# Token columns in tiles of 512, 260 and 260 instead of three of 344, in a two-layer hybrid decoder step

## The reference

```python
def _layer(h, p_l, lst, w, lb, pos, wbuf, prompt):
    u = _rmsnorm(h, w['norm1_g']) @ w['w_in']
    ...
    y_a, h_new, conv_new = _rglru(a_x, a_g, h0, conv0, ...)
    ...
    y_c, s_new = _hgrn2(c_q, c_f, c_i, c_g, lb, s0, w['hgrn_norm_g'])
    y_d, c_new, n_new, m_new = _mlstm(d_q, d_k, d_v, d_o, d_i, d_f, ...)
    h = h + jnp.concatenate([y_a, y_b, y_c, y_d], axis=-1) @ w['w_out']
    f = _rmsnorm(h, w['norm2_g']) @ w['w_up']
    h = h + jnp.square(jax.nn.relu(f)) @ w['w_down']
    h = h + jax.nn.sigmoid(h @ w['w_ple_gate']) * (p_l @ w['w_ple_proj'])
    return h, (h_new, conv_new, k_new, v_new, s_new, c_new, n_new, m_new)
```

## Time and profile before

| | |
|---|---|
| median of 3 runs | 3236.26 us |
| lowest, highest | 3226.01, 3238.97 us |
| span of the profiled execution | 3234.4 us |
| PE busy | 2971.1 us, 92% |
| DVE, ACT, POOL busy | 1149.4, 905.8, 905.2 us |
| chain that ended last | PE 81%, DVE 11%, ACT 3%, no instruction ready (issue) 3% |
| mean granted TensorE clock | 0.935 |

### The profile page before, as it was taken

One profiled execution on the slowest core, in us unless ns is written; L12 is line 12 of the kernel. 1 busy time (PEld: TensorE's weight loads), 2 busy tenths in 40 slices (PEclk: granted clock), 3 DMA queues, 4 the chain that ended last, 5 costly groups with the idle time before them and its releaser, 6 DMA issues.

```text
span 3234.4 us, 43899 instructions
## 1 busy us (share of the span) xinstructions
PE 2971.1 (92%) x18128; PEld 2801.4 (87%) x18128; DVE 1149.4 (36%) x2022; ACT 905.8 (28%) x1377; POOL 905.2 (28%) x591
## 2 busy tenths in 40 slices
PE   5988977889999999999968899778899999999999
PEld 4887865579999999999967788655899999999998
DVE  4643255553222222222355423566422222222223
ACT  4443222233111111113345332223331111111133
POOL 2111244222222332225131112432122223222251
PEclk8999976789999999999979999768899999999999
DMA  4010100021111111112210111000211111111112
GB/s 165 33 48 27 59 20 7 9 88 40 49 50 45 45 45 49 42 46 69 79 59 23 46 41 58 14 1 9 94 44 49 46 45 45 49 48 45 63 52 79
DMA packets 42756, 155.78 MB, mean 48 GB/s; under 512 B 6786, under 2 KB 8066, under 8 KB 41088
## 3 DMA queue, kind: packets, MB, share of 16 engines
q1 hardware_dynamic: 33696, 125.68, 11.3%
q10 hardware_dynamic: 8928, 28.28, 2.3%
HBM read 136.18 MB, written 17.76 MB: 48 GB/s over the span
## 4 chain that ended last, share of the span: by engine, by line
PE 81%; DVE 11%; ACT 3%; issue 3%; POOL 2%; DMA 0%; ACTq 0%; DVEq 0%; SPq 0%; POOLq 0%
PE pj L338 24%; PE pj L339 24%; PE pj L340 24%; DVE small L1648 2%; DVE ext L1334 2%; DVE ext L1843 1%; PE pm L351 1%; DVE small L1334 1%; PE pj L579 1%; DVE vt L1334 1%; PE pm L545 1%; PE pm L430 1%; POOL w_lo L1190 1%; PE pm L549 1%; PE pm L531 1%
## 5 line engine op out<-in xcount | busy, mean ns | idle before, releaser
L338 PE MATMUL pj<-m_hi,w_hi 128*128 128x344 f32 x1920 | 614.4, 320 | 0.0
L340 PE MATMUL pj<-m_hi,w_lo 128*128 128x344 f32 x1920 | 613.2, 319 | 0.0
L339 PE MATMUL pj<-m_lo,w_hi 128*128 128x344 f32 x1920 | 612.7, 319 | 0.0
L338 PE MATMUL pj<-n_hi,w_hi 128*128 128x344 f32 x1584 | 526.5, 332 | 71.9 <-DVE n_lo L1334 27.5
L340 PE MATMUL pj<-n_hi,w_lo 128*128 128x344 f32 x1584 | 516.1, 326 | 0.0
L339 PE MATMUL pj<-n_lo,w_hi 128*128 128x344 f32 x1584 | 516.0, 326 | 0.0
L339 PE MATMUL pj<-hid_lo,w_hi 128*128 128x344 f32 x1536 | 492.9, 321 | 0.0
L338 PE MATMUL pj<-hid_hi,w_hi 128*128 128x344 f32 x1536 | 490.8, 320 | 0.0
L340 PE MATMUL pj<-hid_hi,w_lo 128*128 128x344 f32 x1536 | 490.2, 319 | 0.0
L1243 POOL TENSOR_TENSOR w_lo<-w_raw,w_hi 128x1024 fp32r<-128x1024 f32 x128 | 308.4, 2409 | 628.6 <-ACT w_hi L1082 628.6
L1190 POOL TENSOR_TENSOR w_lo<-w_raw,w_hi 128x1024 fp32r<-128x1024 f32 x84 | 212.1, 2526 | 827.4 <-ACT w_hi L735 827.4
(11 more groups left out here) (330 smaller groups left out, 3430.5 us busy)
## 6 DMA issues: line engine op xcount, KB each, us to landing
w_raw<-in_w SPq DMA_DIRECT2D x216, 512.0 KB, 3.2
out_y<-res ACTq DMA_DIRECT2D x16, 516.0 KB, 2.7
res<-out_y ACTq DMA_DIRECT2D x2, 3096.0 KB, 11.2
res<-in_x SPq DMA_DIRECT2D x4, 1032.0 KB, 8.0
out_y<-res SPq DMA_DIRECT2D x8, 516.0 KB, 15.8
ext<-in_rope SPq DMA_DIRECT2D x2, 1032.0 KB, 12.5
res<-out_y ACTq DMA_DIRECT2D x2, 1032.0 KB, 4.9
hsq<-in_p ACTq DMA_DIRECT2D x2, 1032.0 KB, 4.7
```

The costliest lines, as they stand in the source:

```text
L338: pe.matmul(pj[:, t, 0:TT], wh, hi[:, k, cols], start=(k == 0), stop=False)
L339: pe.matmul(pj[:, t, 0:TT], wh, lo[:, k, cols], start=False, stop=False)
L340: last = pe.matmul(pj[:, t, 0:TT], wl, hi[:, k, cols], start=False, stop=(k == nk - 1))
```

## The change

`TT` goes; `CUT = (0, 512, 772, T)` holds the bounds of the three tiles, `cut(t)` gives a tile's slice and `span_of(t)` its width, 512, 260 and 260 columns. Every place that had `t * TT:(t + 1) * TT` or `0:TT` takes these instead, on all engines. A tile of 512 fills its bank. The number of instructions, their order on each engine, their waits and the DMAs stay.

```diff
-TT = T // 3
+CUT = (0, 512, 772, T)
...
+def cut(t):
+    return slice(CUT[t], CUT[t + 1])
...
+def span_of(t):
+    return CUT[t + 1] - CUT[t]
...
                     for t in range(3):
...
-                        cols = slice(t * TT, (t + 1) * TT)
+                        cols = cut(t)
...
-                            pe.matmul(pj[:, t, 0:TT], wh, hi[:, k, cols], start=(k == 0), stop=False)
-                            pe.matmul(pj[:, t, 0:TT], wh, lo[:, k, cols], start=False, stop=False)
-                            last = pe.matmul(pj[:, t, 0:TT], wl, hi[:, k, cols], start=False, stop=(k == nk - 1))
+                            pe.matmul(pj[:, t, 0:span_of(t)], wh, hi[:, k, cols], start=(k == 0), stop=False)
+                            pe.matmul(pj[:, t, 0:span_of(t)], wh, lo[:, k, cols], start=False, stop=False)
+                            last = pe.matmul(pj[:, t, 0:span_of(t)], wl, hi[:, k, cols], start=False, stop=(k == nk - 1))
...
-                    pe.matmul(pm[:, t, 0:TT], lhs, rhs[:, t * TT:(t + 1) * TT], start=True, stop=True).then_inc(mix_mm, 1)
+                    pe.matmul(pm[:, t, 0:span_of(t)], lhs, rhs[:, CUT[t]:CUT[t + 1]], start=True, stop=True).then_inc(mix_mm, 1)
...
-                    o = dst[out_rows or rows, t * TT:(t + 1) * TT]
-                    act.activation(o, pj[rows, t, 0:TT], func, **kw).then_inc(ev[t], 1)
+                    o = dst[out_rows or rows, CUT[t]:CUT[t + 1]]
+                    act.activation(o, pj[rows, t, 0:span_of(t)], func, **kw).then_inc(ev[t], 1)
```

More of the change, by code:

```diff
@@ L357, in norm @@
                 for t in range(3):
-                    last = pe.matmul(pm[:, t, 0:TT], ones, nrm[:, t * TT:(t + 1) * TT], start=True, stop=added == KT)
+                    last = pe.matmul(pm[:, t, 0:span_of(t)], ones, nrm[:, CUT[t]:CUT[t + 1]], start=True, stop=added == KT)
                     if added == KT:
@@ L364, in norm @@
                 for t in range(3):
-                    pe.matmul(pm[:, t, 0:TT], ones, sqr[:, t * TT:(t + 1) * TT], start=False,
+                    pe.matmul(pm[:, t, 0:span_of(t)], ones, sqr[:, CUT[t]:CUT[t + 1]], start=False,
                               stop=True).then_inc(sems[2], 1)
@@ L578, in mprep @@
                         pe.wait_ge(mp_ev, 3 * (n - 1) + t + 1)
-                    pe.matmul(pj[:, t, 0:TT], sel[at:at + 4, n % 2 * P:(n % 2 + 1) * P],
-                              rows[at:at + 4, t * TT:(t + 1) * TT], start=True, stop=True).then_inc(mp_mm, 1)
+                    pe.matmul(pj[:, t, 0:span_of(t)], sel[at:at + 4, n % 2 * P:(n % 2 + 1) * P],
+                              rows[at:at + 4, CUT[t]:CUT[t + 1]], start=True, stop=True).then_inc(mp_mm, 1)
                 if n == 3:
@@ L767, in factor @@
                     act.wait_ge(sems[2], t + 1)
-                    last = act.activation(nrm[:, t * TT:(t + 1) * TT], pm[:, t, 0:TT], ACT.Ln, bias=EPS, scale=1.0 / D)
+                    last = act.activation(nrm[:, CUT[t]:CUT[t + 1]], pm[:, t, 0:span_of(t)], ACT.Ln, bias=EPS, scale=1.0 / D)
                 last.then_inc(sems[3], 1)
@@ L787, in job @@
                         act.wait_ge(mm[t], 1)
-                        act.activation(slot(8)[0:4, t * TT:(t + 1) * TT], pj[0:4, t, 0:TT], ACT.Copy)
-                        act.activation(slot(9)[0:4, t * TT:(t + 1) * TT], pj[32:36, t, 0:TT],
+                        act.activation(slot(8)[0:4, CUT[t]:CUT[t + 1]], pj[0:4, t, 0:span_of(t)], ACT.Copy)
+                        act.activation(slot(9)[0:4, CUT[t]:CUT[t + 1]], pj[32:36, t, 0:span_of(t)],
                                        ACT.Copy).then_inc(ev[t], 1)
@@ L842, in take_mix @@
                     act.wait_ge(mix_mm, 3 * (n - 1) + t + 1)
[L843 removed]
+                    act.activation(dst[:, CUT[t]:CUT[t + 1]], pm[:, t, 0:span_of(t)], func, **kw).then_inc(mix_ev, 1)
             def gate(_):
@@ L1472, in rope @@
                     for t in range(3):
-                        cols = slice(t * TT, (t + 1) * TT)
+                        cols = cut(t)
                         dve.wait_ge(mix_mm, 3 * (3 + n) + t + 1)
-                        tt(rp_sq[n][:, cols], pm[:, t, 0:TT], slot(19)[:, cols], ALU.mult).then_inc(mix_ev, 1)
+                        tt(rp_sq[n][:, cols], pm[:, t, 0:span_of(t)], slot(19)[:, cols], ALU.mult).then_inc(mix_ev, 1)
                     link(tt(slot(14 + n), slot(14 + n), slot(18), ALU.mult))
@@ L1820, in ff_step @@
                     for t in range(3):
-                        cols = slice(t * TT, (t + 1) * TT)
+                        cols = cut(t)
                         dve.wait_ge(mm[t], i * 12 + (U0 + q + 1))
-                        dve.scalar_tensor_tensor(relu[:, q % 2, cols], pj[:, t, 0:TT], 0.0, nrm[:, cols],
+                        dve.scalar_tensor_tensor(relu[:, q % 2, cols], pj[:, t, 0:span_of(t)], 0.0, nrm[:, cols],
                                                  ALU.max, ALU.mult).then_inc(ev[t], 1)
@@ L1828, in ff_step @@
                     for t in range(3):
-                        cols = slice(t * TT, (t + 1) * TT)
+                        cols = cut(t)
                         dve.wait_ge(mm[t], i * 12 + (U0 + 4 + n + 1))
-                        tt(res[:, n, cols], res[:, n, cols], pj[:, t, 0:TT], ALU.add).then_inc(ev[t], 1)
+                        tt(res[:, n, cols], res[:, n, cols], pj[:, t, 0:span_of(t)], ALU.add).then_inc(ev[t], 1)
             for k in range(KT):
```

2 lines of the change are left out of this document (1 added, 1 removed).

## The result

| | before | after |
|---|---|---|
| median (18 runs each) | 3234.3 us | 3240.1 us |
| lowest, highest | 3223.45, 3239.25 | 3235.43, 3242.61 |
| span of the profiled execution | 3234.4 | 3239.0 |
| mean granted clock | 0.935 | 0.936 |

The ratio is 1.0022, 95% interval 1.0011 to 1.0032: slower by 4 to 10 us, with 5.8 between the medians. That is inside the half per cent and inside the range, but on the other side of the forecast, which was 5.3 us faster. Lines 338 to 340 are now 346 to 348, `mix` is 359, VectorE's helper 1342, ScalarE's takes 750 and 851.

What follows compares the result with a forecast made beforehand. TensorE, busy 92% of the span, was taken to bound the kernel through its matmul spacing; 0 - 3.2 - 0.5 - 0.5 - 1.1 = -5.3 us from 3236.3 gave 3231, range 3168 to 3270.

Steps and rivals of the forecast that it cites:

- the half per cent: Whole kernel: a band of 16 us, about what a measurement can tell; a time within it was given 0.55.
- No change of the bulk: Matmuls of lines 338 to 340: three tiles' matmuls take 472.2 ns at full clock before and after, so 0 us.
- (a): Rival, small tiles: the weight load binds, 123.8 to 126.1 ns per matmul, +14 to +38 us, up to 3269; chance 0.20.
- (b): Rival, full-rate matmuls: 157 ns is a floor, so small tiles still cost 157.4; +299 us, 3530; chance 0.09.
- (c): Rival, wide tile: the excess goes where columns far outlast the load, 215.6 ns, not 227.4; -61 us, 3170; chance 0.15.
- two readings of the excess: Full-clock matmul spacing: the 14.1 ns over a column per cycle grows with columns (0.4576 ns each), or is fixed per matmul.
- First unit of a layer: Behind the wait before k = 7, 3528 fewer columns remain: 1.61 us less, 3.2 us over two layers.
- First unit of `w_out`: Behind its last wait, 504 fewer columns remain: 0.23 us less, 0.5 us over two layers.
- Evictions: Taking tiles from PSUM on VectorE: some 0.69 us for 512 columns, 0.43 for 260, sum unchanged, far from binding.
- the part on order: Where tile order helps: gains behind late operands in first units; 0 for units with a tail of one k.
- The small gains: Shorter last-tile evictions: 0.25 us at each layer's end, 0.5 in all, plus 1.1 us at other row ends.
- The eight places: Per layer, where PE and another engine wait on a row's last tile: 0.07 us each, 1.1 in all.

Runs made afterwards that it cites:

- tail_old: The changed kernel with only the first `w_down` unit of each feed-forward step, the one with the tail, back at 344 columns; 3241.5 us in one run.
- mix_old: The changed kernel with the plain fp32 products (`mix`, `norm`, `mprep`) back at 344 columns; 3233.9 us, ratio 0.9996 to the kernel before.
- ff_narrow: The kernel before with tiles of 260, 260 and 512, widest last, in the feed-forward units alone; 3231.0 us, ratio 0.9986 to the kernel before.
- down_old: The changed kernel with all `w_down` units back at 344 columns; 3238.3 us, ratio 1.0012 to the kernel before.
- first_new: The kernel before with 512, 260, 260 only in each layer's first `w_in` and first `w_out` units; 3235.3 us, ratio 1.0003 to the kernel before.

## Why the prediction was off

**What held.** *No change of the bulk*: 472.5 ns a triple, shown by the spacing and by tail_old. Rivals (a), (b) and (c) are out: 119.9 ns for the small tile is under (a)'s 123.8, 110.5 at 200 columns refutes (b)'s floor of 157, and the wide tile's 232.7 is far from (c)'s 215.6. Of the two readings of the excess the first is nearer: the line through the means of 260 and 512 columns (119.8 and 232.7 ns) is 3.3 + 0.448 ns per column and gives 157.4 and 189.7 for 344 and 416, where 157.5 and 189.8 were measured at full clock. With the wide tile last it is 231 to 232. *First unit of a layer*: 1.61 us forecast; 1.62 and 1.93 in after, 1.6 in each once the difference in half clock is taken off. The time before it was read as 10.8 us and is 10.92. *First unit of `w_out`*: 0.23 us less forecast, and 0.2 less in after; the other profiles moved by -0.3 to +0.1, and the unchanged kernel by -0.2, so it is too small to settle. *Evictions*: 686 and 424 ns.

**The step that failed.** The part on evictions says that "a unit of 24 matmuls a tile gives 5.5 and 2.9 us between them: far from binding", and the part on order counts the units with a tail of one k as "3096 columns either way: 0". The sum of columns is the same, but the question there is how soon a bank is wanted again, and in a unit with a tail that is not 24 matmuls but the six behind tile 0's last. The view for it was at hand: the same place in before's timeline had 0.94 us for an eviction that was 0.51 long. Scaling both ends, 0.72 against 0.69 plus the 0.2 until it starts, would have given the wait. I costed the edit at nothing by an average over ordinary units and did not look at the unit that differs. Measured: 8 x 0.33 in each layer less small gains, 2.1, and 0.34 for the first `w_up` unit: **+5.0 us** over both layers. None of the rivals had this cost in it either. That the measured time lies inside the range of 3168 to 3270 is therefore no merit of the working: the range was made wide for (a) and (c), which are out.

**The mixes were not costed.** They entered the sum only as gains at a row's last tile. Their chains have the same short way round a bank, four instructions or 0.87 us between a wide tile's use and its next: +1.4 to +3.0 us a layer. The upper figure includes a fall of the clock which I would not have foreseen.

**The small gains** (0.25 at a layer's end, eight times 0.07) did not appear as such. The PLE part became 0.2 to 0.3 us longer. I did not take it apart; its projection units are short (nk = 2). The eight places lie in the mixer part, where 0.5 us can't be seen.

**The sum, with what was measured.** From the profile of after: feed-forward with the first `w_up` units and PLE +5.6, first units -3.5, `w_out` of layer 1 and the start -0.5, mixer parts +6.4, norms -3.4: +4.6. The norms' -3.4 is one of clock: PE has 11.4 us less half clock there. It is there too in mix_old and ff_narrow, where `norm` has tiles of 344, and missing in tail_old and down_old, where it has the wide one; so it is no property of the tiles in `norm`. The final norm in before, then in after:

```profile
3224.17 2.66 PE L358 MATMUL pm<-small,cst 128*128 128x344 f32 x6 [2.79 <-DVE small L1334]
3226.63 2.97 PE L365 MATMUL pm<-small,cst 128*128 128x344 f32 x6
```

```profile
3230.07 2.00 PE L366 MATMUL pm<-small,cst 128*128 128x512 f32 x6 [2.70 <-DVE small L1342]
3231.91 1.90 PE L373 MATMUL pm<-small,cst 128*128 128x512 f32 x6
```

What decides where these stretches begin stays open. It is what keeps the mixer part's share of the 6 us from being split more finely than: feed-forward +5.0 (its loop shown by removal), first units -3.2 without the clock's share (shown alone in first_new), the mixes +1.4 to +3.0 a layer, read from chains and in line with mix_old's ratio.

## What to carry to other kernels

PSUM banks that are used in turn form a ring: each is wanted again after one round. When the tiles in it become unequal, look for the shortest way round, not for the average unit: the wide bank must be emptied while only the small tiles run, so the time allowed shrinks just where the eviction grows. A unit that finishes its last k for all tiles together, and a chain of short products, are such places. If operands arrive late in tile 0 put the wide tile first; if the banks come round quickly put it last; the two can be chosen unit by unit.

## What the runs showed of the hardware

- The spacing of fp32r matmuls at full clock, each with a load of its own, was 119.8, 157.5, 189.8 and 232.7 ns for 260, 344, 416 and 512 columns: 0.448 ns a column, 7.5% more than one column per cycle at 2.4 GHz, and 3.3 ns. At 200 columns it was 110 to 111 ns, about the load's 112. At half clock it is columns/1.2: 286.7 ns for 344, 346.6 for 416, 427 for 512.
- A wait of PE for a bank cost 0.11 us more than its length in all 16 steps of after: the load behind it starts with its matmul and not before.
- Two profiled executions of the unchanged kernel differ by 5.7 us, with 10.4 us less at half clock in the shorter one and nothing over 0.1 us apart where the clock was 1.00. Where the granted clock was 0.57 and not 1.00 over 174 to 178, dense matmuls took 1.55 us longer; at 0.66 over 149 to 154, where PE waits anyway, nothing was lost. A gain of under some 3 us can't be read from such a part; in the feed-forward loop, where the clock was 1.00 throughout, 0.1 us could.
